# Right operands of matmuls moved to 64 bytes below the weights modulo 512, and the experts' first products as three matmuls of 256 columns

## What is computed

```python
for l in range(2):                      # first block
    h = rms_norm(x, g1) * (1 + scale1) + shift1      # modulated by c
    z = h @ w_in[l]                     # attention, gated convolution and pooling parts
    x = x + gate1 * (mix @ w_out[l])
    h2 = rms_norm(x, g2) * (1 + scale2) + shift2
    x = x + gate2 * peer_ffn(h2, ...)   # 16384 experts, 8 heads, top 16 each
# peer_ffn
q = ht @ w_q;  top-k of q against two sets of 128 keys -> eidx, gate
act = gelu(einsum('td,thkd->thk', ht, expert_u[eidx]), approximate=False)
y   = einsum('thk,thkd->td', gate * act, expert_v[eidx])
# second block
x = x + concat(s5_mixer(...), ssd_mixer(...)) @ w_out
x = x + cross_attention(rmsnorm(x), rmsnorm(mem), wq, wk, wv, wo)
x = x + (silu(conv(g)) * v) @ w_down    # [g, v] = rmsnorm(x) @ w_up, width 2816
out = rmsnorm(x)
```

## Time and profile before

| | us |
|---|---|
| median of 3 runs (2447.69 to 2451.53) | 2449.75 |
| the profiled execution's own time | 2447.19 |
| its span in the profile | 2445.4 |
| TensorE busy, matmuls | 2371.1 (97%) |
| VectorE busy | 1769.0 (72%) |
| ScalarE busy | 1165.0 (48%) |
| GpSimd busy | 148.7 (6%) |

### The profile page before, as it was taken

How to read it: one execution, slowest core, us unless ns; L and a number is a source line. 1 busy time by engine, 2 the same in 40 slices (tenths; PEclk the granted TensorE clock), 3 DMA queues, 4 the chain that set the end, 5 groups by cost and what they waited for, 6 DMA issues and landing times. The chain is left out here.

```text
span 2445.4 us, 37022 instructions
## 1 busy us (share of the span) xinstructions
PE 2371.1 (97%) x14412; PEld 2124.7 (87%) x14412; DVE 1769.0 (72%) x2947; ACT 1165.0 (48%) x1715; POOL 148.7 (6%) x205
## 2 busy tenths in 40 slices
PE   5989999999999999999999999999999999999998
PEld 5889898888888888889899888888888888998998
DVE  7989887676767676678978676566767566655665
ACT  4542355444545454564145544455545523545544
POOL 0000352000000000000055000000000000000000
PEclk9989999999999999999999999999999999999999
DMA  9365435786666666434534686665555523343553
GB/s 357 141 228 164 147 130 165 270 292 241 232 240 232 240 232 223 149 110 148 178 120 138 203 309 210 212 207 189 189 189 189 189 79 105 129 148 135 184 189 104
DMA packets 133556, 460.66 MB, mean 188 GB/s; under 512 B 15152, under 2 KB 16432, under 8 KB 132912
## 3 DMA queue, kind: packets, MB, share of 16 engines
q1 hardware_dynamic: 133424, 458.90, 55.0%
HBM read 445.73 MB, written 13.11 MB: 188 GB/s over the span
## 5 line engine op out<-in xcount | busy, mean ns | idle before, releaser
L1691 DVE TENSOR_TENSOR ring_lo<-ring,ring_hi 128x1024 fp32r<-128x1024 f32 x421 | 507.0, 1223 | 86.1 <-ACT ring_hi L1594 86.1
L1594 ACT ACTIVATE ring_hi<-ring 128x1024 fp32r<-128x1024 f32 x421 | 434.9, 1053 | 132.4 <-PE banks L346 119.4
L319 PE MATMUL banks<-normed_lo,ring_hi 128*128 128x512 f32 x1344 | 477.9, 398 | 0.0
L344 PE MATMUL banks<-ring_hi,work_lo 128*128 128x512 f32 x1024 | 400.4, 391 | 6.5 <-PEq L1187 3.7
L345 PE MATMUL banks<-ring_lo,work_lo 128*128 128x512 f32 x1024 | 399.9, 391 | 0.0
L346 PE MATMUL banks<-ring_hi,work_lo 128*128 128x512 f32 x1024 | 399.1, 390 | 0.0
L320 PE MATMUL banks<-normed_lo,ring_lo 128*128 128x256 f32 x1344 | 377.2, 281 | 0.0
L319 PEld LDWEIGHTS banks<-normed_lo,ring_hi 128*128 128x128 f32 x1344 | 252.5, 188 | 61.7
L361 DVE TENSOR_TENSOR ring_lo<-ring,ring_hi 128x1024 fp32r<-128x1024 f32 x185 | 225.0, 1223 | 73.3 <-ACT ring_hi L356 72.8
L320 PEld LDWEIGHTS banks<-normed_lo,ring_lo 128*128 128x128 f32 x1344 | 253.8, 189 | 3.3
L356 ACT ACTIVATE ring_hi<-ring 128x1024 fp32r<-128x1024 f32 x185 | 194.8, 1055 | 94.2 <-PE banks L311 53.5
(11 more groups left out here) (401 smaller groups left out, 4396.4 us busy)
## 6 DMA issues: line engine op xcount, KB each, us to landing
ring<-wstream SPq DMA_DIRECT2D x716, 512.0 KB, 3.5
arena<-wstream SPq DMA_DIRECT2D x96, 512.0 KB, 5.3
spill<-one_hots SPq DMA_DIRECT2D x44, 256.0 KB, 4.2
rstd<-spill SPq DMA_DIRECT2D x16, 256.0 KB, 3.7
pool_and_keys<-spill SPq DMA_DIRECT2D x14, 256.0 KB, 3.8
routes<-spill SPq DMA_DIRECT2D x14, 256.0 KB, 4.6
residual<-xT SPq DMA_DIRECT2D x1, 1024.0 KB, 8.2
arena<-mixconst SPq DMA_DIRECT2D x2, 512.0 KB, 4.9
```

Source lines behind the costliest of these rows:

```text
L319: pe.matmul(dst, w_hi[:, o], HR[:, k, :], start=(k == 0), stop=(k == KD - 1), skip_group_check=True)
L344: pe.matmul(dst, hi[:, t], w_hi[:, o], start=first, stop=False)
L1594: sc.activation(RING_HI[:, u % HIGHS, :], RING[:, u % SLOTS, :], ACT.Copy)\
L1691: dve.tensor_tensor(RING_LO[:, u % SLOTS, :], RING[:, u % SLOTS, :], RING_HI[:, u % HIGHS, :].bitcast(F32), ALU.subtract).then_inc(S("spli ...
```

## The change

Two parts. First, placement: layer vectors and modulation, with a pad of 8 elements, are allocated ahead of "normed", and a pad of 16 elements behind it. `Arena.passing` moves a cut to 448 bytes modulo 512, and is called ahead of MIX, of the second block's scan tensors and its MIX, of cross attention's tensors and of F. Second, the expert loop's first products are made by `unit_product`, three matmuls of 256 columns per chunk, the two units of a pair in the two halves of one bank; `unit_halves`, `cross_terms` and `join` go, and the gelu reads the bank.

```diff
         RING, RING_LO = two("ring", [P, SLOTS, D])
+        LVS = sb("layer_vectors", [P, DEPTH, L_COLS])
+        MOD = sb("modulation", [P, 48])
+        sb("pad_normed", [P, 8])
         HF, HR = two("normed", [P, KD, 2 * T])
+        sb("pad_work", [P, 16])
...
-        LVS = sb("layer_vectors", [P, DEPTH, L_COLS])
         PK = sb("pool_and_keys", [P, 512])
-        MOD = sb("modulation", [P, 48])
...
+            def passing(self):
+
+                self.at += (112 - self.at) % 128
...
             PL = a(2, T)
+            a.passing()
             MIX, MIX_LO, MIX_HI = a.split(8, T)
...
-                            unit_halves(pe, PS[:, 2 * bank + e, :], S_EXP + i + e)\
+                            unit_product(pe, PS[:, bank, e * T:(e + 1) * T], S_EXP + i + e, H_HI, H_LO)\
                                 .then_inc(units_used, 1)
...
-                            pe.wait_ge(S("joined"), j - AHEAD)
+                            pe.wait_ge(S("gelu_done"), j - AHEAD)
...
-                    def cross_terms(q, done):
+                    def gelu(q, done):
 
                         sc.wait_ge(units_used, done)
-                        sc.activation(E[:, q, :].rearrange("p (e t) -> p e t", e=2), PS[:, 2 * q:2 * q + 2, T:2 * T],
-                                      ACT.Copy).then_inc(S("cross_copied"), 1)
-
-                    def gelu(j, q):
-
-                        sc.wait_ge(S("joined"), j + 1 - AHEAD)
-                        sc.activation(E[:, q, :], E[:, q, :], ACT.Gelu).then_inc(S("gelu_done"), 1)
+                        sc.activation(E[:, q, :], PS[:, q, :], ACT.Gelu).then_inc(S("gelu_done"), 1)
...
-                        cross_terms(q, r * SLOTS + (S_EXP + i))
+                        gelu(q, r * SLOTS + (S_EXP + i))
                         high(2 + i, r)
-                        gelu(j, q)
...
-                    def join(j, q):
-
-                        dve.wait_ge(S("cross_copied"), j + 1 - AHEAD)
-                        both = E[:, q, :].rearrange("p (e t) -> p e t", e=2)
-                        dve.tensor_tensor(both, PS[:, 2 * q:2 * q + 2, 0:T], both, ALU.add).then_inc(S("joined"), 1)
-
...
         DEC = a(12)
+        a.passing()
         seg_at = a.at
...
         SYQ = a(6, T)
+        a.passing()
         mix_at = a.at
...
         a.at = keep
+        a.passing()
         MEM = a(8, T)
...
         CV = a(2, T)
+        a.passing()
         F, F_LO, F_HI = a.split(2, T)
```

More of the change, by code:

```diff
@@ L311, in unit_product @@
                 mm = pe.matmul(dst, w_lo[:, o], hi[:, k, :], start=False, stop=(k == KD - 1))
[L312 to L321, removed]
             return mm
@@ L1662, in _ @@
                     high(6, 31)
-                    cross_terms(1, S_EXP + 252)
-                    gelu(63, 1)
+                    gelu(1, S_EXP + 252)
                     high(7, 31)
@@ L1734, in step @@
                         j, i = r * 2 + q, 4 * q
-                        join(j, q)
                         low(2 + i, r)
@@ L1868, in _ @@
                             v(dve.tensor_tensor(S1G[:, o:o + 8], S1G[:, o:o + 8], after[:, g:g + 8], ALU.mult), "mod")
-                    join(63, 1)
                     low(6, 31)
```

## The result

The kernel after the change takes 2439.01 us (median of 5 runs, 2434.54 to 2441.18) against 2451.53 for the kernel before (5 runs, 2447.69 to 2456.3): ratio 0.9939, 95% interval 0.9924 to 0.9954. That is 12.5 us or 0.6% faster, where 37.8 us were forecast. The time lies above the top of the range, 2431.

A forecast was written before the change was run, and what follows sets the result against it. TensorE, busy for 97% of the span, was taken as the bound, through its pace of passes. Terms of 14.0, 6.7, 4.2, 5.4, 3.9 and 3.6 sum to 37.8 us: 2447.2 to 2409.4, by the median 2412 us; range 2400 to 2431.

The forecast's parts named there:

- 18 passes take 2.04 us, 113.3 ns each: Feed-forward's down products, from their seventh pass on: the pace read from the trace, against 119.6 ns for the up products.
- so all 256-column fp32r passes come to where F is: Placement step: operands move to 448 modulo 512, where hidden operand F lies; 113.6 ns a pass taken instead of 119.6.
- two controls at offset 0: Grouped products (changing destination every three passes) and mixer operands (in the arena): both at 120 ns, leaving offset as F's reason.
- The loop, 14.0 forecast: Expert loop's first products: 48 passes at 113.6 ns, 0.167 us gained a step over 84 steps; bounds 8.5 lost, 17.0 gained.
- rival 1: Placement does nothing, F's pace is its own; the loop's third pass costs 8.5 us, 2458 us in all; chance 0.09.
- sum of low bounds: Whole kernel: all terms at their low bounds, the loop at 12, give a gain of 29 us, so 2421 us.
- The feed-forward, 6.7 forecast: Feed-forward up products: 1056 passes at 6.0 ns less give 6.3 us, settling no longer there 0.4; down products unchanged.
- The query stage, 4.2 forecast: Query products: 768 passes at 6.0 ns would give 4.6 us; VectorE's load limits it to 4.2, bound 3.6.
- The early expert products, 5.4 forecast: Early expert products: 1200 passes in short runs, 1072 of them gaining 5 ns each; bounds 2 and 6.4 us.
- Mixers and second block, 7.5 forecast together: Mixers' in and out products 3.9 us (bounds 2 and 6.3), second block's products 3.6 us (bounds 2.5 and 4.2).
- rival 2: Outside loop and feed-forward, TensorE's gain goes into waits for VectorE, ScalarE or norms; gain 20.7 us, 2429 us; chance 0.12.
- Rival 3: Loop's 256-column passes go below 113.3 ns, toward 107; another 18.5 us, as much elsewhere at most, 2375 to 2394; chance 0.09.

The follow-up runs named there:

- e12_off0_cut: e2_three with the last 512-column pass of each step's second products cut into two of 256 columns, operands at offset 0: 2463.21 us, ratio 1.0048.
- e5_map: TensorE alone runs streams of 256- and 512-column passes at offsets 0 to 480 bytes, reference's work left out: 256-column passes 120.0 ns at 0, 117.8 or 113.3 at 448.
- e8_off288: Kernel after the change, with the passing operands at 288 bytes (32 modulo 256) instead of 448: 2437.35 us, ratio 0.9936.
- e2_three: Kernel before the change, with three 256-column passes per chunk in the loop's first products and operands left at offset 0: 2464.89 us, ratio 1.005.
- e9_wide256: Kernel after the change, with the last 512-column pass of each step's second products cut into two of 256 columns: 2418.5 us, ratio 0.9853.
- e11_same: Kernel after the change, unchanged and profiled once more: a span of 2432.1 us against 2439.4 in the first profile.
- e1_place: Kernel after the change, with the loop's first products as before (512- and 256-column pass per chunk, copy and join kept): 2440.79 us, ratio 0.9941.

## Why the prediction was wrong

**The step that failed** is "18 passes take 2.04 us, 113.3 ns each", carried over as "so all 256-column fp32r passes come to where F is", at 113.6 ns. The offset was the right cause: two controls at offset 0 held, and e12_off0_cut, e5_map and e8_off288 confirm that the pace goes by placement. But 113.3 is one of two paces there. I read one run of down products (2307.84) out of 22, took its pace as the offset's own, and put the slower first six passes down to settling. The first run, at 2256.98, showed 117.8 for as long as it lasted.

**The loop, 14.0 forecast, 1.1 came.** It is entered behind the second products, and there always at the slow pace: 48 x 117.8 = 5.653. By e2_three and after the terms are: the third pass costs 0.112 us a step, the placement at the slow pace gives back 0.099, and the second products gain 0.027. The result lies between the term's two bounds, but neither stood for it: the low one (119.6) was rival 1's, the high one 113.3. In the sum of low bounds the loop stood at a gain of 12, for which no row was given; with 1.1 in its place that sum is 18 and not 29. (The terms' high bounds add up to 44.8, not 43.) With the quick pace the term was right: e9_wide256 gains 0.187 us a step and 14.95 in all.

**The feed-forward, 6.7 forecast.** 0 by whole pairs in the profile of after, since up gained 0.09 us and down lost 0.09 in each. From its first up pass to the start of its last down pass the stage took 190.6 us before, 191.5 in after and 185.2 in e11_same, the last two with 4.4 us for the first run of down products, in part at half clock, where before needed 2.9; e9_wide256, quick and without that fall, took 183.6, 7.0 less than before. The term was right for an execution that is quick throughout. What I had not thought of at all was the loss: down products that get slower at an unchanged placement, by my reading because their stream now runs on from the up products' without a change of offset and takes over their pace (argued, not tested).

**The query stage, 4.2 forecast.** The pairs are 0.09 and 0.29 us shorter in turn, a mean of 0.19, over 16 pairs 3.0 us. VectorE did not get in the way.

**The early expert products, 5.4 forecast.** The 1200 passes, summed start to start, take 154.6 us against 157.5: 2.9. Mixers and second block, 7.5 forecast together: start to start, the arena operands' 960 passes fell from 119.2 to 116.0 us, the normed ones outside loop, query and feed-forward by 1.4, so 4.6. All other matmuls, waits included, grew from 571.5 to 574.9, so part of this went into waits, as rival 2 has it; I did not test which. The sum of these terms is 1.1 + 0 + 3.0 + 2.9 + 4.6 - 3.4 = 8.2, against 6.0 between the two profiled spans (2445.4 and 2439.4): the loop and the feed-forward summed with their first and last units lose 0.7 and 0.9 where their whole steps gain 1.1 and 0, which makes 5.5 of the 8.2. With the span of e11_same (2432.1) it is 13.3, nearer to the 12.5 of the medians.

**What held.** Join and cross copies are gone and no wait of TensorE for gelu appears; VectorE fell by 54.1 us (58 forecast). Gelu from the bank takes 598 ns (50.2 us for 84), as the copy did. ScalarE fell by 34.5 on the page, not by 50: 84 activations (52.2 us) are gone, and the durations of its instructions summed fall by 51.3, but they overlap and the page counts each moment once. That costing these at nothing was right is seen in e2_three, which drops the copies and joins at the old placement: its second products stay at 5.468 us (5.467 before) and its first ones at 48 x 119.8. And e1_place, which keeps them all, is as quick as after.

**The rivals.** Rival 1 (placement does nothing) is refuted by e1_place against before, but its price for the third pass was right: 9.3 measured in the 82 steps of e2_three for 8.5. Its remark that "no first product at 448 is in the trace" was the open point, and deserved a case of its own: first products at 448, at a pace between the two. Rival 2 (2429) is nearer to the median than the forecast by luck, since 14.0 of its 20.7 us lay in the loop, which gave 1.1. Rival 3 (below 113.3) did not occur: in no kernel did 24 such passes in a row go under 113.3. The offset that counts is taken modulo 256, not 512; 448 and 192 are one case, so nothing in the forecast hung on it.

**The rule.** With three passes throughout, placement is worth 26 us (2464.89 against 2439.01), and 45 with the cut (2463.21 against 2418.5), of which the loop's 82 steps hold 10.4 and 25.3, and e5_map shows 120 against 113.3 ns with TensorE alone. The Trainium skill, page "TensorE: Matmul & The Clock Gate", Part 2, says that loading the next tile's weights doesn't steal read bandwidth from the running matmul. By that rule all offsets would have one pace; the measurement disagrees by up to 6.7 ns a pass, and decides. The Trainium skill's page "SBUF — State Buffer", section "Who interferes with whom", is not contradicted by this, since that is about other engines, and none was at work.

**What stays open.** What it is in an entry that chooses. It is not the code alone (e11_same, and the query stage's turns), and the query stage's regular turns suggest that the choice of one stream reaches over the short break to the next one. Why the distance counts, and why with a period of 256 bytes, is not visible in any of these traces; that two reads meet in SBUF is a guess. Which pace the unprofiled executions of each kernel had is not known either.

## What to carry to other kernels

Before a pace from one place of a trace is carried to another, read every stretch that has the same placement, the first and the odd ones above all: one stretch at another pace means a second condition. TensorE's streams of 256-column fp32r passes here depend on the distance between passing and loaded operand modulo 256 bytes, and at the best distance on how they are entered; a pass cut in two at the entry gave 13.85 us in the loop beyond the change, and cost 0.04 us a step (10.92, where first and second products at their best, 5.44 each, would take 10.88). Passes of 512 columns are quickest at distance 0, so one placement does not serve both. When two executions of one program differ, compare the granted clock and the pace stage by stage before the difference is put down to the code.

## What the runs showed of the hardware that I had not expected

- Two stable paces at one placement, 113.3 and 117.8 ns, held for as long as the streams here lasted (the loop's 48, the feed-forward's 20 pairs of 72 one behind the other).
- What looks like a memory through breaks: in the query stage identical pairs take turns, 6.55 and 6.35 us, with eight other matmuls between them.
- A stream that was at 113.3 ns came back at 117.8 behind a stretch at half clock (after, from 2253.95 us on), and elsewhere at 113.3 (e11_same).
- A period of 256 bytes in the offset, with 116.7 (32), 117.8 (64), 120.0 (0, 96) among its values.
- Another order for 512 columns: 226.7 ns at offset 0, where 256 columns are slowest, and 233.3 with the passing operand 64 bytes below (e5_map).
- An operand that isn't touched by an edit can lose by it: the down products, 2.74 to 2.83 us a run, in the executions in which the stream arrives at the slow pace.
